# Rows of 29 experts gathered one expert sooner into six buffers; the last expert's gathers and sums in the next block; feature copies with the Fourier stage

## The reference, cut to what matters

```python
def expert_block(args):
    xblk, e = args
    gu = xblk @ w_gu[e] + b_gu[e]
    gate, up = jnp.split(gu, 2, axis=-1)
    gate = jnp.minimum(gate, SWIGLU_LIMIT)
    up = jnp.clip(up, -SWIGLU_LIMIT, SWIGLU_LIMIT)
    act = (up + 1.0) * gate * jax.nn.sigmoid(SWIGLU_ALPHA * gate)
    return act @ w_down[e] + b_down[e]
...
y = zeros.at[buf_tok].add(yb * buf_w[:, None])
...
h = h + g2 * moe(modulate(rmsnorm(h, norm_mlp_w[l]), sh2, sc2), ...)
return rmsnorm(h, final_norm_w)          # end of the first block
...
h = rms_norm(x, norm_g)                  # the second block's first layer
proj = h @ w_in
f_in, f_gate, q, k, v, a_gate = jnp.split(proj, EVEN_SPLITS, axis=-1)
```

## Time and profile before

| | us |
|---|---|
| median of 3 runs | 2349.99 |
| lowest, highest | 2348.99, 2350.17 |
| profiled execution, its own time | 2349.28 |
| span of its profile | 2347.0 |
| TensorE busy | 2210.5 (94%) |
| VectorE busy | 780.9 (33%) |
| ScalarE busy | 470.0 (20%) |
| GpSimd busy | 144.8 (6%) |

### The profile page before, as it was taken

The page is one execution under the profiler, slowest core; times in us unless marked ns, Lnnn a source line. Parts: engine busy times, 40 slices in busy tenths (PEclk is TensorE's granted clock), DMA queues, the critical chain, the costliest instruction groups (busy, mean ns, idle before and its releaser), DMA issues. The chain is left out here.

```text
span 2347.0 us, 35635 instructions
## 1 busy us (share of the span) xinstructions
PE 2210.5 (94%) x14438; PEld 905.5 (39%) x14438; DVE 780.9 (33%) x1411; ACT 470.0 (20%) x837; POOL 144.8 (6%) x174
## 2 busy tenths in 40 slices
PE   5999886999999999999999983999999998999998
PEld 2434541333333333333333321455445444444443
DVE  1133447522222222222222244003077003456543
ACT  2121222111011111001111102110126002446530
POOL 0000002101111101111101031000000000000000
PEclk9999997999999999999999996999999999999999
DMA  9138528999999999999999984113210221122210
GB/s 364 54 114 308 210 95 338 391 414 417 416 416 415 416 414 417 417 416 414 415 416 416 415 306 165 54 54 101 89 54 1 72 72 45 54 90 90 72 36 36
DMA packets 144126, 557.13 MB, mean 237 GB/s; under 512 B 19397, under 2 KB 34926, under 8 KB 110178
## 3 DMA queue, kind: packets, MB, share of 16 engines
q1 hardware_dynamic: 118998, 513.20, 55.4%
q0 software_dynamic: 11472, 30.31, 3.6%
q10 hardware_dynamic: 13596, 12.80, 1.6%
HBM read 539.58 MB, written 25.03 MB: 241 GB/s over the span
## 5 line engine op out<-in xcount | busy, mean ns | idle before, releaser
L1952 PE MATMUL ps<-ring,xeT 128*32 128x512 f32 x6144 | 669.6, 595 | 4.9 <-ACT xeT L1553 4.9
L1952 PEld LDWEIGHTS ps<-ring,xeT 128*32 128x32 f32 x6144 | 196.3, 110 | 450.6 <-issue 444.1
L1922 PE MATMUL ps<-ring,mT 128*32 128x512 f32 x2048 | 267.9, 595 | 8.1 <-DVE mT L1762 8.1
L1672 ACT ACTIVATE mT<-mT 128x768 f32<-128x768 f32 x32 | 27.0, 843 | 898.6 <-DVE mT L1748 898.6
L1748 DVE TENSOR_SCALAR mT<-ps 128x768 f32<-128x768 f32 x32 | 30.6, 957 | 488.8 <-PE ps L1952 488.8
L360 PE MATMUL ps<-hT_late,ring 128*128 128x512 f32 x384 | 167.6, 599 | 4.5 <-PEq L2218 4.5
L1930 PE MATMUL ps<-ring,mT 128*32 128x256 f32 x2048 | 157.7, 380 | 0.0
L1930 PEld LDWEIGHTS ps<-ring,mT 128*32 128x32 f32 x2048 | 66.3, 110 | 154.7 <-issue 154.7
L2897 PE MATMUL ps<-hT_late,ring 128*128 128x512 f32 x256 | 110.6, 592 | 1.3 <-PEq L2656 1.3
L360 PEld LDWEIGHTS ps<-hT_late,ring 128*128 128x128 f32 x384 | 73.8, 193 | 97.5 <-issue 97.5
L360 PE MATMUL ps<-ring,mT 128*128 128x512 f32 x256 | 110.1, 592 | 1.2 <-PEq L2463 1.2
(11 more groups left out here) (399 smaller groups left out, 2038.9 us busy)
## 6 DMA issues: line engine op xcount, KB each, us to landing
ring<-in_w_gu SPq DMA_DIRECT2D x256, 1024.0 KB, 8.6
ring<-in_w_down SPq DMA_DIRECT2D x128, 1024.0 KB, 7.9
ring<-in_even_w_in SPq DMA_DIRECT2D x18, 1024.0 KB, 7.4
ring<-in_w_ada SPq DMA_DIRECT2D x32, 512.0 KB, 6.4
ring<-in_odd_w_in SPq DMA_DIRECT2D x32, 512.0 KB, 5.4
ring<-in_w_ada SPq DMA_DIRECT2D x8, 1024.0 KB, 20.8
ring<-in_w_in SPq DMA_DIRECT2D x8, 1024.0 KB, 15.3
y_scratch<-ysb ACTq DMA_DIRECT2D x128, 64.0 KB, 4.7
```

Of the source, the lines that this page charges most:

```text
L1672: nc.scalar.activation(sig[:, 0:W], gate[:, 0:W], ACT.Sigmoid, scale=1.702).then_inc(M.sig_ready, 1)
L1922: mm = nc.tensor.matmul(quad(b, 2 * q + n), acted(k, q, src), w[:, kk, n * BANK:(n + 1) * BANK], start=first, stop=last)
L1952: mm = nc.tensor.matmul(quad(q, c), left(q), part_columns(w, c), start=start, stop=stop)
```

## The change

`BEFORE` goes from 30 to 29, so the sixteen gathers need experts 0 to 28 only, and may start one expert sooner; experts 29, 30 and 31 have four gathers each. There are six buffers, two more in the part of `mT` where the last expert's rows went. VectorE's loop ends one expert earlier; expert 30's step is written out and has four sums between its product and its transposition, the other twelve follow it. The sums for expert 29 stand behind expert 31's transposition, those for expert 30 at the start of the norm block; expert 31's gathers are in the norm block too, into ring slots that are free then. SyncE loads `w1b` behind the last expert weights and stores the last third of experts 30 and 31. The norm block's buffers now lie in `mT`. ScalarE's feature copies and VectorE's writing of `res` move into the Fourier stage's block. The path for surplus tokens gets other buffers.

```diff
-        last_rows = mT[:, KD:, :].rearrange("p (t h) n -> p t (h n)", t=NT)
+        w1b = mT[:, KD:KD + 2, :].rearrange("p k n -> p (k n)")
...
-        GB = 4
-        gbuf = hT[:].rearrange("p (b k) n -> p b (k n)", b=GB)
-        BEFORE = E - 2
...
+        xrow = scratch[:, 0:D]
+        last_rows = scratch[:, 4096:].rearrange("p (t n) -> p t n", t=NT)
+        gbuf = [buf[:, 2 * b:2 * b + 2, :].rearrange("p k n -> p (k n)") for buf, b in
+                [(hT, b) for b in range(4)] + [(mT, KD // 2 + 1), (mT, KD // 2 + 3)]]
+        GB = len(gbuf)
...
+        BEFORE = E - 3
...
+        def sum_rows(dve, n0, n1):
+            for n in range(n0, n1):
+                i, t = divmod(n - NT * TOPK, NT)
+                w = w_end[:, i, t:t + 1] if i >= 0 else w_early[:, n:n + 1]
+                if i < 0:
+                    t = n // TOPK
+                dve.wait_ge(rowed[n % GB].sem, 16 * (n // GB + 1))
+                if n:
+                    row_used.wait(dve)
+                row_used.on(nc.vector.scalar_tensor_tensor(out=res[:, t, :], in0=gbuf[n % GB], scalar=w, in1=res[:, t, :],
+                                                           op0=ALU.mult, op1=ALU.add))
...
                 stream.loaded = moe0 + SLOTS + 12 * (E - 2)
+                stream.load(sp, end_moe - 7)
+                sp.wait_ge(parted.sem, 4)
+                w1b_loaded.on(sp.dma_start(w1b, A["final_norm_w"].rearrange("(a n) -> a n", a=1).to_broadcast([P, D])), 16)
+                for e in (E - 2, E - 1):
+                    sp.wait_ge(M.y_read, e + 2)
+                    for c in range(4):
+                        part = slice(c * QUAD, (c + 1) * QUAD)
+                        sp.dma_start(y_rows(e, 2, 4, c), ysb[part, Q2]).then_inc(M.y_stored, 16)
                 stream.load(sp, end_moe)
-                sp.wait_ge(M.y_read, E + 1)
-                for c in range(4):
-                    part = slice(c * QUAD, (c + 1) * QUAD)
-                    sp.dma_start(y_rows(E - 1, 2, 4, c), ysb[part, Q2]).then_inc(M.y_stored, 16)
...
-                pool.wait_ge(M.y_stored, 128 * (BEFORE + 1))
-                for n in range(NT * TOPK + NT):
+                for n in range(NT * TOPK + 2 * NT):
+                    i, t = divmod(n - NT * TOPK, NT)
+                    after = max(i, -1) + 1
+                    if n == 0 or n >= NT * TOPK and t == 0:
+                        pool.wait_ge(M.y_stored, 128 * (BEFORE + 1 + after))
                     if n >= GB:
                         pool.wait_ge(row_used.sem, n - GB + 1)
-                    if n == NT * TOPK:
-                        pool.wait_ge(M.y_stored, 128 * (BEFORE + 2))
-                    at = dest[:, n:n + 1] if n < NT * TOPK else idx_end[:, 0, n - NT * TOPK:n - NT * TOPK + 1]
-                    end = (BEFORE if n < NT * TOPK else BEFORE + 1) * CAP
+                    at = idx_end[:, i, t:t + 1] if after else dest[:, n:n + 1]
+                    end = (BEFORE + after) * CAP
                     rowed[n % GB].on(nc.gpsimd.indirect_dma_start(
-                        gbuf[:, n % GB, :], None, y_dram[0:end, :], bass.IndirectOffsetOnAxis(ap=at, axis=0),
-                        bounds_check=end - 1, oob_is_err=False), 16)
-                pool.wait_ge(M.y_stored, 128 * (E + 1))
-                for t in range(NT):
-                    last_rowed[t].on(nc.gpsimd.indirect_dma_start(
-                        last_rows[:, t, :], None, y_dram[0:E * CAP, :],
-                        bass.IndirectOffsetOnAxis(ap=idx_end[:, 1, t:t + 1], axis=0), bounds_check=E * CAP - 1,
+                        gbuf[n % GB], None, y_dram[0:end, :], bass.IndirectOffsetOnAxis(ap=at, axis=0), bounds_check=end - 1,
                         oob_is_err=False), 16)
...
-                        store(e)
+                        store(e, third=not last)
...
                     nc.vector.tensor_tensor(up[:, 0:W], up[:, 0:W], sig[:, 0:W], ALU.mult).then_inc(M.act_ready, 1)
                     dve.wait_ge(M.act_ready, e + 1)
+                    if between:
+                        between()
                     if last:
                         nc.vector.transpose(last_turned[:, 0:W], up[:, 0:W]).then_inc(M.aT_read, 1)
                         return
...
-                with dve.Fori(0, E - 3) as i:
+                with dve.Fori(0, E - 4) as i:
                     prepare(i + 2)
                     block_step(i + 2, False)
...
-                sum_rows(0, 2 * TOPK)
+                bias_added.wait(dve)
+                prepare(E - 2)
+                block_step(E - 2, False, between=lambda: sum_rows(dve, 0, TOPK))
+                sum_rows(dve, TOPK, NT * TOPK)
                 block_step(E - 1, False, last=True)
-                sum_rows(2 * TOPK, 3 * TOPK)
+                sum_rows(dve, NT * TOPK, NT * TOPK + NT)
                 dve.wait_ge(M.y_done, 2 * (E - 1))
                 read_y(E - 1, Y0)
-                sum_rows(3 * TOPK, NT * TOPK)
                 dve.wait_ge(M.y_done, 2 * E)
                 read_y(E, Y0 + 2)
-                sum_rows(NT * TOPK, NT * TOPK + NT)
...
             @block.sync
             def _(sp):
-                w1b_loaded.on(sp.dma_start(w1b[:], A["final_norm_w"].rearrange("(a n) -> a n", a=1).to_broadcast([P, D])), 16)
                 for t in range(NT):
-                    last_rowed[t].wait(sp)
+                    sp.wait_ge(rowed[t].sem, 16 * 5)
                 stream.load(sp, end_moe + 1, LATE_SLOTS)
+            @block.gpsimd
+            def _(pool):
+                pool.wait_ge(M.y_stored, 128 * (E + 1))
+                for t in range(NT):
+                    rowed[t].wait(pool)
+                    rowed[t].on(nc.gpsimd.indirect_dma_start(
+                        last_rows[:, t, :], None, y_dram[0:E * CAP, :],
+                        bass.IndirectOffsetOnAxis(ap=idx_end[:, 2, t:t + 1], axis=0), bounds_check=E * CAP - 1,
+                        oob_is_err=False), 16)

             @block.vector
             def _(dve):
                 def join(t):
-                    last_rowed[t].wait(dve)
-                    h_ready.on(nc.vector.scalar_tensor_tensor(out=res[:, t, :], in0=last_rows[:, t, :], scalar=w_end[:, 1, t:t + 1],
+                    rowed[t].wait(dve)
+                    h_ready.on(nc.vector.scalar_tensor_tensor(out=res[:, t, :], in0=last_rows[:, t, :], scalar=w_end[:, 2, t:t + 1],
                                                               in1=res[:, t, :], op0=ALU.mult, op1=ALU.add))
                     h_ready.wait(dve)
-                    h_ready.on(nc.vector.tensor_tensor(hw[:, t, :], res[:, t, :], w1b[:], ALU.mult))
+                    h_ready.on(nc.vector.tensor_tensor(hw[:, t, :], res[:, t, :], w1b, ALU.mult))

...
+                sum_rows(dve, NT * TOPK + NT, NT * TOPK + 2 * NT)
+                row_used.wait(dve)
                 w1b_loaded.wait(dve)
                 join(0)
...
                 scale(3)
-                for t in range(NT):
-                    nc.vector.tensor_scalar(res[:, t, :], hw[:, t, :], pair[:, t, 2:3], None, ALU.mult)
...
                 root(NT - 1)
-                act_features(act, j_ev, "even_norm_2")
...
             @block.scalar
             def _(act):
+                act_features(act, j_ev, "even_norm_2")
                 for i, j in enumerate(j_fi):
                     j.filled(act)
                     j.empty(nc.scalar.activation(fT[:, i, :], bank(j.bank), ACT.Copy))
+                act.wait_ge(h_ready.sem, 3 * NT)
...
             @block.vector
             def _(dve):
+                for t in range(NT):
+                    h_ready.on(nc.vector.tensor_scalar(res[:, t, :], hw[:, t, :], pair[:, t, 2:3], None, ALU.mult))
```

More of the change, by code:

```diff
@@ L1452, in build @@
         xval = sbuf("xval", [P, 2, XB], scope=moe_scope)
-        xw = hT[:].rearrange("p (i k) n -> p i (k n)", i=2)
-        GB = 4
-        gbuf = hT[:].rearrange("p (b k) n -> p b (k n)", b=GB)
-        BEFORE = E - 2
+        xw = scratch[:, 4096:].rearrange("p (i n) -> p i n", i=2)
+        xrow = scratch[:, 0:D]
[4 more added lines that the diff above has]
+        BEFORE = E - 3
+        w1b_loaded = signal("w1b_loaded")
         rowed = [signal(f"rowed{b}") for b in range(GB)]
-        last_rowed = [signal(f"last_rowed{t}") for t in range(NT)]
         row_used = signal("row_used")
@@ L1560, in pass_on @@
             nc.gpsimd.tensor_tensor(mark[:], ident[:, 0:1], ident[:, 0:1], ALU.mult).then_inc(S.marked, 1)
-        M = Expert(*[sem(f"moe_{name}") for name in EXPERT_SIGNALS])
+        M = Expert(*[sem(f"moe_{name}") if name != "up_done" else None for name in EXPERT_SIGNALS])
         buffers_zero = amat_zero.n + 2
@@ L1744, in prepare, with block_step @@
                     dve_onehot(dve, M, lambda t: place[:, t, bass.ds(e + 3, 1)], lambda t: third_of[:, t, bass.ds(e + 3, 1)])
-                def block_step(e, first, last=False):
+                def block_step(e, first, last=False, between=None):
```

(17 more changed lines are left out.)

32 lines of the change are left out of this document (9 added, 23 removed).

## The result

The changed kernel takes 2334.31 us (median of 4 runs, 2331.08 to 2335.03) against 2349.49 us for the kernel before in the same comparison: ratio 0.9933, interval [0.9915, 0.9950], about 15 us or 0.7% faster. The forecast was 2323 us with a range of 2317 to 2333. The direction was right; the gain was little more than half of the 27 us.

A forecast was written before the change was run, and what follows sets the result against it. TensorE, busy 94% of the span, was taken as the bound, so only its gaps could be gained. Terms -9.8 - 14.7 + 1.5 - 3.3 - 1.0 = -27.3 us took 2349.28 to 2322.0, stated as 2323 us, range 2317 to 2333.

The forecast's parts named there:

- Term A: Before the last down projection: early gathers remove TensorE's 8.09 us wait and the 1.74 us slow start, -9.83 us.
- the limit of 1382.9: Latest end of the early sums on VectorE for expert 31's transposition to be done when TensorE needs it at 1387.79.
- first rival: Early gathers come too late because weights hold the transfer engines; the -9.8 us gain becomes about 0, time 2333; chance 0.11.
- No wait for `ring` between 1356 and 1398: Expert block: a TensorE wait for weights at its ring in that time would have shown the forecast wrong.
- fourth rival: Gathers hold weights past their 23.9 us lead, TensorE stalls in experts 30 and 31; 2355 us or more; chance 0.03.
- Term B: End of the expert block: TensorE's end to the norm block's start falls from 22.80 to 8.1 us, -14.7 us.
- Term C: Norm block start: the 3.87 us norm weight wait goes, four moved sums add 5.4 us; first join later, +1.5 us.
- Term D: Between transposes and first projection: feature copies leave the block's end, so 4.47 us becomes 1.2, -3.3 us.
- Term E: Projection's start: the clock may stay up over the shorter gap; between 0 and -1.4 us, taken as -1.0.

The follow-up runs named there:

- second profile of the changed kernel: The changed kernel unaltered, profiled again when timed beside two later runs against the kernel before: 2333.70 us, ratio 0.9938.
- the two kernels with both repairs: Changed kernel with expert 31's step after the twelfth sum, and the next stage's first tile requested between SyncE's stores or in the next block: 2323.53 and 2322.00 us.
- the kernel with the tile in the next block: Changed kernel with expert 31's step after the twelfth sum and the next stage's first weight tile requested only in the next block: 2322.00 us, ratio 0.9886.

## Why the prediction was wrong, step by step

**Term A, -9.8 us: failed, +1.2 measured.** The failing step is the prediction's "The first gather of before took 6.8 us to its sum ... I take that for each". It used the time of a first gather for each of sixteen beside a saturated stream, as if they had no rate. Measured where weights are moved, a gather took 13.9 to 15.7 us from issue to landing with six under way, and, whatever that time, one came every 2.7 us. The sixteenth sum ended at 1391.9, 9 us behind the limit of 1382.9. The working of the first rival had the right test, 2.47 us per gather until the limit, but two of its numbers were off. A gather is 0.50 MB, not 0.43: the fourteen of the earlier trace rows were counted as they were issued, and the last of them had not moved their bytes by 1400. And half the engines was taken to mean half the bytes. The Trainium skill's rule ("DMA: Bandwidth & Descriptors", "Queues, rings and completion order": queues with work are served in turn, packet by packet) agrees with 1078 and 1077 packets and with 391 and 391. What I drew from it does not: shares in bytes go with the size of the packets, 136 GB/s and 33.8% of the engines beside packets of 7.2 KB, 181 GB/s and 45.2% beside those of 3.8 KB. Even at the 197 GB/s of the prediction, 0.50 MB are 2.5 us, past the limit. The first rival's mechanism, A at zero because weights hold the engines, is what happened; it deserved far more than 0.11. That its 2333 us lies so near 2334.31 is in part luck, since B, the transposes and E were off as well and partly cancel (below). Its argument against, that four sums ran back to back before, came from a time when the weights had ended: before, their queue still had 64.9% of the engines from 1370 to 1375, and moved nothing from 1375 to 1380.

That the late gate is all that A lost is shown twice over: by taking bytes away (9.9 us), and by moving the gate ahead of the last sums with the bytes as they are (9.0 us). In the second, TensorE doesn't wait although the transfers are as slow: they cost because all sixteen sums were put ahead of the gate.

**The weights: right.** No wait for `ring` between 1356 and 1398. The fourth rival did not occur, with less to spare than the forecast took: in the second profile of the changed kernel the last eight tiles took 23.3 us to land in the median, 8.0 before, of a lead of 31.9.

**Term B, -14.7: -10.3 measured.** The step that failed is "With 3.1 us behind GpSimd's last gather"; it was 6.93 (6.06 in the second profile), which is 3.8 of the missing 4.4 us; the last gather itself ended 3.7 us behind TensorE's end instead of 3.2. I had written of the tile behind the stores that nobody needs it before 1430. Nobody does, but the last gather's packets shared the engines with it, and the barrier waits for that landing. Without the tile it was 2.97 and, in the two kernels with both repairs, 3.3. From TensorE's end to VectorE's first sum, the kernel with the tile in the next block takes 1406.99 - 1397.76 = 9.2 us, near the 8.1 of the forecast. The experiment that undid the last gathers' move shows the part of B that this move carries: 3.4 us.

**Term C, +1.5: right for the join, +1.6.** The first join is 5.5 us after the norm block's first sum (3.87 before); the wait for `w1b` is gone. From the join to the end of the last scaling it is 15.1 us, as forecast. The transposes behind it cost another 0.7 us that stands in no term: the last 24 took 5.38 us instead of 4.65, at a granted clock of 0.50 until 1445, where the earlier trace rows had a mean of 0.81 under the last of them.

**Term D, -3.3: right.** Last transposes to first projection: 4.47 us before, 1446.10 - 1444.96 = 1.1 now.

**Term E, -1.0: too small.** Between the projection's start and the request for `dft_c` another 12.4 - 10.0 = 2.4 us came in: the granted clock was 1.00 from 1446 on. The copies did not pace the projection noticeably (TensorE busy 1.90 of the 2 us from 1446). D and E together were undone in one experiment: 5.0 us in the medians; in its trace 3.74 - 1.13 = 2.6 us for D and (1466.71 - 1451.01) - (1460.10 - 1446.10) = 1.7 us for E, 4.3 together, where before and after differ by 5.7.

**The sum.** 27.3 less A (9.8 + 1.2 of loss), less the missing part of B (4.4), less C and the transposes (0.9), plus the excess of E (1.4), is 12.4, what the two traces show at the request for `dft_c`. The other 1.9 of the 14.3 us came in the stages behind, which the forecast put at nothing; their cause stays open. With A's place and B's tile repaired the kernel takes 2322 us, the forecast's number, and here the steps agree too: TensorE's end at 1397.76 (forecast 1398.3), the norm block at 1406.99 (1406.4), the first projection at 1431.20 (about 1430). The forecast was thus a fair size of what this rearrangement gives once both faults are repaired, and a wrong statement of what this version of it does.

## What to carry to other kernels

A transfer that starts sooner also starts into other traffic: price a row of transfers by bytes over the share that its queue can get there, not by the time from issue to use of the first one. Gathered work belongs behind the step for which the busy engine waits, where the order of the waiting engine's queue allows it. A transfer that nobody needs yet, asked for at a block's end, can delay the one that the barrier waits for.

## What the runs showed that was not expected

- Two queues with work moved packets one for one (391 and 391 in 10 us, 1078 and 1077 in 20 us), so the queue with packets of 7.2 KB had 67.7% of the engines and that of 3.5 KB 33.8%.
- Rows that the bounds leave out of a gather still cost a packet: with about half the rows a gather took 2.3 us instead of 2.7, while its bytes fell from 181 to 2.76/25 = 110 GB/s.
- TensorE's granted clock rose to 1.00 in the gap of 1.1 us between the transposes and the projection (mean of 1445 to 1446: 0.72) and stayed there. With a gap of 3.7 us it had risen too (1.00 from 1448 to 1451) but fell behind the projection's start, to 0.50 from 1452 to 1454.
